# Last two blocks' outputs of an expert layer added through one-hot products, and the third output tile added onto a preset shift in memory

## Chip, cores and metric

The kernel runs on one core of a Trainium2 chip. The metric is the device time of one execution in microseconds (us), as the median of three runs. TensorE (PE) does the matrix products, VectorE (DVE), ScalarE (ACT) and GpSimd (POOL) the rest; SyncE (SP) issues most DMAs, POOL the indirect and the accumulating ones.

## What is computed

One step of a one-layer hybrid decoder over 512 prompt tokens and 8 sample tokens (520 rows, model width 2048), in float32. The part that matters is the end: a mixture of experts with two experts per token, and the last LayerNorm.

```python
h = silu(einsum('td,edf->tef', xf, w_gate)) * einsum('td,edf->tef', xf, w_up)
y = einsum('tef,te,efd->td', h, gate, w_down)
out = layer_norm(ALPHA * x1 + y, ln2_g, ln2_b)
```

## The kernel before

**Stages.** First comes the input projection with attention, recurrence and convolution beside it (lines 1805 and on), then the output projection, which ends in the first LayerNorm and the routing near 850 us, then the experts. The token rows chosen for one expert are cut into blocks of 128. A loop over blocks `j` gathers 128 rows, turns them, multiplies them with 8 tiles of gate and up weights and, one block later, with 4 tiles of down weights. In this run there are 17 blocks; in the code `last` is 16 and `nb` is 17. The last two blocks are written out behind the loop: `gate_up(last)`, then `down_column` four times for the block before, then four times for the last one, each for 512 of 2048 output columns.

**Precision.** A float32 product is made of three products of fp32r operands: each operand is split into a high part, which ACT writes (`bhi`, line 1050), and a low part, the difference, which DVE writes (`blo`, line 1683). Weights come by SP into `RAWB` (six slots of 1 MB, lines 602 and 682); SP reuses a slot when DVE has made the low part.

**Adding the outputs up.** `y_rows` is a table in device memory of 520 rows, preset with the scaled residual (line 659). After each block ACT copies the four finished PSUM banks to `YO` (line 1071), and POOL adds the 128 rows to their places in `y_rows` with one indirect accumulating DMA (line 768). For the second to last block this is done in four quarters of 512 columns, each as soon as it is copied (line 804). The last block's rows are not scattered: ACT copies them to `YO2`; DVE makes one-hot matrices `OWN` (lines 1737 to 1740) that say which output row each of the 128 rows belongs to; and PE multiplies `OWN` with `YO2` in plain float32 (lines 2266, 2268, 2275), which spreads the rows over the 512 prompt rows, in four tiles of 128, and over the 8 sample rows.

**The end.** SP waits for all scatters (line 704), then loads `y_rows` as four tiles `X2` of 1 MB (line 707) and the sample rows `X8` (line 709). Ahead of that it has loaded the LayerNorm rows, scale `LG2` and shift `LB2`, each as two DMAs of 64 partitions (lines 697 and 698), and `LG8`, `LB8` (line 701); all six DMAs count on one semaphore, `f_ln`, for which DVE waits before `centred(0)`. Per tile DVE adds the PE product to `X2` and sums the row (`added`, line 1767), ACT makes the mean (`mean`, line 1152), DVE subtracts it and applies the scale (`centred`, line 1772), ACT squares and sums (`squares`, line 1156) and takes the root (line 1157), and DVE inverts it (`root`, line 1776). Tiles 0 and 1 (`NACC = 2`) are finished by ACT (`scaled`, line 1161) and added by POOL onto output rows which SP has preset with the shift during the output projection (lines 624 and 625, accumulating DMA line 817). Tiles 2 and 3 are finished by DVE (`finished`, line 1785) and written plainly by SP (line 717). The sample rows take a side path through `Z8` and `z_rows` (lines 1144, 712, 714) and are written last (lines 1760, 719). Every engine takes its instructions in the order written; DMAs of one queue move in the order issued.

Of the kernel before, what the change touches and what calls it, by code (L numbers as in the profile page):

```python
# [16 lines left out]
D = 2048  # L17
# [97 lines left out]
def build(nc, a, o):  # L115
# [9 lines left out]
    y_quarters = y_rows.rearrange("t (c n) -> (t c) n", c=4)  # L125
# [93 lines left out]
    NF, NACC = 4, 2  # L219
# [5 lines left out]
    YO2 = sb("YO2", [128, D], F32, O_M + 8192)  # L225
    HTH2 = sb("HTH2", [128, 4, 128], F32R, O_M)
    HTL2 = sb("HTL2", [128, 4, 128], F32R, O_M + 2048)
    OWN = sb("OWN", [128, NF, 128], F32, O_M + 34816)
# [6 lines left out]
    OWN8 = sb("OWN8", [128, DB], F32, O_8 + 3584)  # L235
    TOKF = sb("TOKF", [128, 1], F32, O_8 + 3648)
# [28 lines left out]
    with ExitStack() as ctx:  # L265
# [165 lines left out]
        YIX4 = small("YIX4", [128, 4], I32)  # L431
# [33 lines left out]

        def last_bank(k, n):

            return ((0, 1, 2, 3), (6, 7, 4, 5))[k % 2][n]

        DOWN_BANK, LAST_DOWN_BANK = (2, 4, 5, 7), (0, 1, 3, 6)  # L470
# [20 lines left out]
        def _(sp):  # L491
# [160 lines left out]
            nb = sp.value_load(EBI[0:1, 31:32], min_val=7, max_val=MAXB - 2) + 2  # L652
# [40 lines left out]

            for k, (t, w) in enumerate(((LG2, "ln2g"), (LB2, "ln2b"))):
                sp.wait_ge(b_lo[k], 4 * nb - 1)
                passed(sp)
                sp.dma_start(t[0:64, :], a[w][0:64, :]).then_inc(f_ln, 16)
                sp.dma_start(t[64:128, :], a[w][0:64, :]).then_inc(f_ln, 16)
            sp.wait_ge(s_y0, 16 * NT)
            for t, w in ((LG8, "ln2g"), (LB8, "ln2b")):  # L700
                sp.dma_start(t[:, :], a[w][0:4, :].rearrange("r (c n) -> (r c) n", c=32)).then_inc(f_ln, 16)

            sp.wait_ge(f_out, 32 * NACC)
            sp.wait_ge(b_yw, 16 * nb + 48)
            passed(sp)
            for i in range(NF):
                sp.dma_start(X2[:, i, :], y_rows[128 * i:128 * i + 128, :]).then_inc(f_in[i], 16)
            in8 = "(g r) (c n) -> (r c) g n"
            sp.dma_start(X8[:, :, :], y_rows[SEQ:T, :].rearrange(in8, g=2, c=32)).then_inc(f_in8, 16)
# [17 lines left out]
        def _(pool):  # L727
# [17 lines left out]
            last_quarter = pool.to_reg(4 * T - 1)  # L745
# [72 lines left out]
            pool.wait_ge(b_yw, 16 * nb + 48 + 16 * NACC)  # L818
# [4 lines left out]
        def _(act):  # L823
# [312 lines left out]
            for n in range(1, 3):
                column_copy(n, n, nb, YO2, LAST_DOWN_BANK)
            act.activation(MV2[:, 0, 3:4], EPS_LN2, ACT.Sqrt)
            column_copy(3, 3, nb, YO2, LAST_DOWN_BANK)


            def samples_copy(n):
                act.wait_ge(f_p, 5 + n)
                act.activation(Z8[:, 512 * n:512 * n + 512], BANK[0:DB, last_bank(1, n), :], ACT.Copy).then_inc(b_y, 1)

            def samples_sd():
                act.wait_ge(f_t8, 2)
                act.activation(S8[:, 4:6], BANK[:, 7, 2:4], ACT.Sqrt, bias=EPS_LN2, scale=1.0 / D).then_inc(f_v8, 1)
# [26 lines left out]
            samples_sd()
# [3 lines left out]
        def _(dve):  # L1179
# [532 lines left out]
            with dve.Fori(1, MAXB) as j:  # L1712
                with dve.If(j < last):
# [653 lines left out]
```

## Time and profile before

| | |
|---|---|
| median of 3 runs | 1498.01 us (1496.25 to 1498.43) |
| profiled execution, its own time | 1493.46 us |
| span of the profiled execution | 1491.6 us |
| PE, DVE, ACT, POOL busy | 96%, 68%, 52%, 13% of the span |
| chain that ended last | PE 85%, DVE 7%, DMA 3%, ACT 2% |
| granted PE clock, mean | 0.982 |

The span runs from the first to the last instruction; the profiled execution's own time lies 1.9 us above it. The chain is the work that ended last, followed back from the end. PE holds it nearly throughout; the other shares gather at the stage borders and behind the last weight product. All stretches below are in us from the span's start.

### The profile page before, as it was taken

The page shows a single profiled execution, that of the slowest core. Times are in us where ns is not written, and L with a number is a line of the kernel's source. Part 1 is how long each engine was busy: PE and PEld are TensorE (multiplying, and loading weights), DVE is VectorE, ACT ScalarE, POOL GpSimd, SP SyncE. Part 2 cuts the span into 40 slices and gives each one's busy share as a digit, 9 for nine tenths or more (in the row PEclk, how much of TensorE's full clock was granted, in tenths as well). Part 3 has the DMA queues.
Part 4 walks back from the last instruction along what each step waited for, and adds up shares of the span by engine and source line. Part 5 has one row for each costly group of instructions (what it writes and reads, how often), then busy time and mean ns, then how long its engine had stood idle before and what let it go on. Part 6 is the DMA issues. An engine that isn't in the chain of part 4 may idle for free.

```text
span 1491.6 us, 24267 instructions
## 1 busy us (share of the span) xinstructions
PE 1439.3 (96%) x9396; PEld 1291.7 (87%) x9396; DVE 1015.0 (68%) x1287; ACT 770.8 (52%) x912; POOL 190.4 (13%) x99
## 2 busy tenths in 40 slices
PE   8999999999999999999997999999999999999995
PEld 7999999999999999999996467888888888888772
DVE  4246746757777787523125668888888888888877
ACT  4245545444434433411110047777777777777774
POOL 0000000000000000234330001121121211222130
PEclk9999999999999999999998899999999999999998
DMA  7321231322213312633435699999999999999997
GB/s 262 123 89 57 86 114 61 96 90 86 88 57 115 116 58 73 205 111 146 145 96 205 207 394 375 384 401 391 392 375 384 384 382 398 387 390 401 348 294 232
DMA packets 74389, 335.36 MB, mean 225 GB/s; under 512 B 12086, under 2 KB 18790, under 8 KB 45514
## 3 DMA queue, kind: packets, MB, share of 16 engines
q1 hardware_dynamic: 68842, 315.54, 56.2%
q0 software_dynamic: 5472, 18.74, 5.0%
q8 instruction: 56, 0.92, 0.2%
q14 instruction: 19, 0.16, 0.0%
HBM read 313.56 MB, written 40.73 MB: 238 GB/s over the span
## 4 chain that ended last, share of the span: by engine, by line
PE 85%; DVE 7%; DMA 3%; ACT 2%; issue 2%; POOL 0%; ACTq 0%; SPq 0%; DVEq 0%; POOLq 0%
PE BANK L1811 13%; PE BANK L1812 13%; PE BANK L1813 13%; PE BANK L2170 7%; PE BANK L2172 7%; PE BANK L2171 7%; PE BANK L2222 4%; PE BANK L2220 4%; PE BANK L2221 4%; PE BANK L2154 2%; DMA RAWB<-in_w_up 2%; PE BANK L2183 2%; PE BANK L1953 1%; PE BANK L1829 1%; PE BANK L2050 1%
## 5 line engine op out<-in xcount | busy, mean ns | idle before, releaser
L1811 PE MATMUL BANK<-XH,HI 128*128 128x260 f32 x1746 | 503.0, 288 | 1.4 <-DVE RT L1487 1.0
L1683 DVE TENSOR_TENSOR LOB<-RAWB,HIB 128x2048 fp32r<-128x2048 f32 x196 | 448.6, 2291 | 74.0 <-ACT HIB L1050 73.1
L1812 PE MATMUL BANK<-XL,HI 128*128 128x260 f32 x1746 | 495.3, 284 | 0.0
L1813 PE MATMUL BANK<-XH,LO 128*128 128x260 f32 x1746 | 494.3, 283 | 0.0
L1050 ACT ACTIVATE HIB<-RAWB 128x2048 fp32r<-128x2048 f32 x196 | 376.4, 1921 | 86.0 <-PE BANK L2172 66.1
L1811 PEld LDWEIGHTS BANK<-XH,HI 128*128 128x128 f32 x1746 | 331.2, 190 | 2.7 <-issue 1.7
L1812 PEld LDWEIGHTS BANK<-XL,HI 128*128 128x128 f32 x1746 | 331.1, 190 | 0.7
L1813 PEld LDWEIGHTS BANK<-XH,LO 128*128 128x128 f32 x1746 | 330.9, 190 | 0.0
L2170 PE MATMUL BANK<-HIB,XGH 128*128 128x512 f32 x512 | 201.8, 394 | 5.5 <-issue 3.0
L2172 PE MATMUL BANK<-LOB,XGH 128*128 128x512 f32 x512 | 200.0, 391 | 0.0
L2171 PE MATMUL BANK<-HIB,XGL 128*128 128x512 f32 x512 | 199.8, 390 | 0.0
L836 ACT ACTIVATE HI<-RAW 128x2048 fp32r<-128x2048 f32 x55 | 105.1, 1911 | 146.5 <-PE BANK L1813 139.6
L731 POOL TENSOR_TENSOR LO<-RAW,HI 128x2048 fp32r<-128x2048 f32 x14 | 66.1, 4721 | 713.5 <-ACT HI L836 713.5
L1198 DVE TENSOR_TENSOR LO<-RAW,HI 128x2048 fp32r<-128x2048 f32 x41 | 93.8, 2289 | 42.9 <-ACT HI L836 42.6
L2170 PEld LDWEIGHTS BANK<-HIB,XGH 128*128 128x128 f32 x512 | 96.7, 189 | 26.2 <-DVE LOB L1683 3.3
L2172 PEld LDWEIGHTS BANK<-LOB,XGH 128*128 128x128 f32 x512 | 96.5, 188 | 20.5
L1487 DVE SCALAR_TENSOR_TENSOR RT<-RT,BANK 128x260 f32<-128x260 f32 x32 | 13.5, 424 | 147.3 <-PE BANK L1813 147.3
L2171 PEld LDWEIGHTS BANK<-HIB,XGL 128*128 128x128 f32 x512 | 96.6, 189 | 19.5
L2220 PE MATMUL BANK<-HIB,HTH 128*128 128x512 f32 x240 | 99.4, 414 | 0.0
L2222 PE MATMUL BANK<-LOB,HTH 128*128 128x512 f32 x240 | 94.7, 395 | 0.0
L2221 PE MATMUL BANK<-HIB,HTL 128*128 128x512 f32 x240 | 93.6, 390 | 0.0
L768 POOL DMA_INDIRECT y_rows<-YO,YIXC x15 | 37.4, 2495 | 355.3 <-ACT YO L1071 355.3
(388 smaller groups left out, 1674.5 us busy)
## 6 DMA issues: line engine op xcount, KB each, us to landing
RAWB<-in_w_down SPq DMA_DIRECT2D x68, 1024.0 KB, 9.5
RAWB<-in_w_gate SPq DMA_DIRECT2D x67, 1024.0 KB, 9.4
RAWB<-in_w_up SPq DMA_DIRECT2D x67, 1024.0 KB, 8.9
RAW<-in_w_in SPq DMA_DIRECT2D x39, 1024.0 KB, 4.9
RAW<-in_w_out SPq DMA_DIRECT2D x16, 1024.0 KB, 5.0
Y<-in_xT SPq DMA_DIRECT2D x8, 520.0 KB, 9.1
RT<-in_xT SPq DMA_DIRECT2D x16, 260.0 KB, 5.2
x_rows<-R SPq DMA_DIRECT2D x5, 832.0 KB
```

The lines of the kernel that those rows point to most:

```text
L836: act.activation(HI[:, u % 2, :], RAW[:, u % 2, :], ACT.Copy).then_inc(s_hi, 1)
L1050: act.activation(HIB[:, s, :], RAWB[:, r, :], ACT.Copy).then_inc(b_hi, 1)
L1683: dve.tensor_tensor(LOB[:, s, :], RAWB[:, r, :], HIB[:, s, :].bitcast(F32), ALU.subtract).then_inc(b_lo[s], 1)
L1811: pe.matmul(bank, hw[:, c, :], h, start=(c == 0), stop=False)
L1812: pe.matmul(bank, hw[:, c, :], l, start=False, stop=False)
L1813: ins = pe.matmul(bank, lw[:, c, :], h, start=False, stop=(c == KC - 1))
L2170: pe.matmul(b, XGH[:, cc, :], hw[:, c, :], start=(cc == 0), stop=False)
L2171: pe.matmul(b, XGL[:, cc, :], hw[:, c, :], start=False, stop=False)
L2172: ins = pe.matmul(b, XGH[:, cc, :], lw[:, c, :], start=False, stop=(cc == KC - 1))
L2220: pe.matmul(b, th[:, c, :], hw[:, m, :], start=(c == 0), stop=False)
L2221: pe.matmul(b, tl[:, c, :], hw[:, m, :], start=False, stop=False)
L2222: ins = pe.matmul(b, th[:, c, :], lw[:, m, :], start=False, stop=(c == 3))
```

## The change

The last two blocks no longer differ: both outputs are split into high and low parts (`YAH`, `YAL` for the second to last, `YBH`, `YBL` for the last), and PE adds both through one-hot matrices `OWN[0]` and `OWN[1]`, which are now fp32r, with four fp32r products for each 512 columns. POOL's four quarter scatters go. DVE gets eight `out_lo` subtractions and a second set of one-hot matrices. SP loads `X2` and `X8` right behind the last weight tile, after a wait for the last scatter of the loop alone, and the LayerNorm rows after them. `NACC` is 3: output tile 2 too is preset in the output projection (one more pair of lines 624 and 625, with n = 9), scaled by ACT and added by POOL. The order of the last steps changes on PE, ACT and DVE. PSUM banks of the spread products are the down banks.

```diff
@@ -216,24 +215,27 @@
-    NF, NACC = 4, 2
+    NF, NACC = 4, 3
...
-    YO2 = sb("YO2", [128, D], F32, O_M + 8192)
+    YAH = sb("YAH", [128, D], F32R, O_M + 8192)
+    YAL = sb("YAL", [128, D], F32R, O_M + 16384)
+    YBH = sb("YBH", [128, D], F32R, O_M + 24576)
+    YBL = sb("YBL", [128, D], F32R, O_M + 32768)
...
-    OWN = sb("OWN", [128, NF, 128], F32, O_M + 34816)
+    OWN = [sb(f"OWN{x}", [128, NF, 128], F32R, O_M + 4096 + 2048 * i) for i, x in enumerate("AB")]
...
-    OWN8 = sb("OWN8", [128, DB], F32, O_8 + 3584)
-    TOKF = sb("TOKF", [128, 1], F32, O_8 + 3648)
+    OWN8 = [sb(f"OWN8{x}", [128, DB], F32R, O_8 + 3584 + 32 * i) for i, x in enumerate("AB")]
+    TOKF = sb("TOKF", [128, 2], F32, O_8 + 3648)
@@ -463,11 +464,11 @@
+DOWN_BANK, LAST_DOWN_BANK, STAT_BANK = (2, 4, 5, 7), (0, 1, 3, 6), 0
...
-    return ((0, 1, 2, 3), (6, 7, 4, 5))[k % 2][n]
...
-DOWN_BANK, LAST_DOWN_BANK = (2, 4, 5, 7), (0, 1, 3, 6)
+    return (DOWN_BANK, LAST_DOWN_BANK)[k % 2][n]
@@ -691,33 +693,31 @@
+    sp.wait_ge(s_y0, 16 * NT)
+    sp.wait_ge(b_yw, 16 * last)
...
+    for i in range(NF):
+        sp.dma_start(X2[:, i, :], y_rows[128 * i:128 * i + 128, :]).then_inc(f_in[i], 16)
+    in8 = "(g r) (c n) -> (r c) g n"
+    sp.dma_start(X8[:, :, :], y_rows[SEQ:T, :].rearrange(in8, g=2, c=32)).then_inc(f_in8, 16)
...
-    sp.wait_ge(s_y0, 16 * NT)
...
-    sp.wait_ge(f_out, 32 * NACC)
-    sp.wait_ge(b_yw, 16 * nb + 48)
...
-    for i in range(NF):
-        sp.dma_start(X2[:, i, :], y_rows[128 * i:128 * i + 128, :]).then_inc(f_in[i], 16)
-    in8 = "(g r) (c n) -> (r c) g n"
-    sp.dma_start(X8[:, :, :], y_rows[SEQ:T, :].rearrange(in8, g=2, c=32)).then_inc(f_in8, 16)
...
-    for k, (i, c0, n) in enumerate(((2, 0, D), (3, 0, D // 2), (3, D // 2, D // 2))):
+    for k, (i, c0, n) in enumerate(((3, 0, D // 2), (3, D // 2, D // 2))):
...
-    sp.wait_ge(f_out, 32 * NACC + 16 * (NF - NACC + 1) + 16)
+    sp.wait_ge(f_out, 32 * NACC + 32 * (NF - NACC) + 16)
@@ -788,23 +787,6 @@
-    pool.wait_ge(b_yw, 16 * last)
...
-    pool.tensor_copy(YIXC[:, :], YIX[:, bass.ds(last - 1, 1)]).then_inc(b_iy, 1)
-    pool.wait_ge(b_iy, last)
...
-    for n in range(4):
-        ins = pool.tensor_scalar(YIX4[:, n:n + 1], YIXC[:, :], 4, n, ALU.mult, ALU.add)
-    ins.then_inc(b_iy, 1)
-    pool.wait_ge(b_iy, last + 1)
...
-    for n in range(4):
-        pool.wait_ge(b_y, 4 * last - 1 + n)
...
-        pool.indirect_dma_start(
-            out=y_quarters, out_offset=bass.IndirectOffsetOnAxis(ap=YIX4[:, n:n + 1], axis=0),
-            in_=YO[:, 512 * n:512 * n + 512], in_offset=None,
-            bounds_check=last_quarter, oob_is_err=False, compute_op=ALU.add).then_inc(b_yw, 16)
@@ -815,7 +797,7 @@
-    pool.wait_ge(b_yw, 16 * nb + 48 + 16 * NACC)
+    pool.wait_ge(b_yw, 16 * last + 16 * NACC)
@@ -1121,31 +1103,31 @@
-    act.wait_ge(b_yw, 16 * last)
-    column_copy(0, 8, last)
+    column_copy(0, 8, last, YAH)
...
-    column_copy(1, 9, last)
+    column_copy(1, 9, last, YAH)
...
-    column_copy(2, 10, last)
+    column_copy(2, 10, last, YAH)
...
-    column_copy(3, 11, last)
+    column_copy(3, 11, last, YAH)
...
-    column_copy(0, 0, nb, YO2, LAST_DOWN_BANK)
+    act.wait_ge(b_yw, 16 * last)
+    column_copy(0, 0, nb, YBH, LAST_DOWN_BANK)
...
     for n in range(1, 3):
-        column_copy(n, n, nb, YO2, LAST_DOWN_BANK)
+        column_copy(n, n, nb, YBH, LAST_DOWN_BANK)
...
-    column_copy(3, 3, nb, YO2, LAST_DOWN_BANK)
+    column_copy(3, 3, nb, YBH, LAST_DOWN_BANK)
...
     def samples_copy(n):
-        act.wait_ge(f_p, 5 + n)
-        act.activation(Z8[:, 512 * n:512 * n + 512], BANK[0:DB, last_bank(1, n), :], ACT.Copy).then_inc(b_y, 1)
+        act.wait_ge(f_p, 9 + n)
+        act.activation(Z8[:, 512 * n:512 * n + 512], BANK[0:DB, last_bank(2, n), :], ACT.Copy).then_inc(b_y, 1)
...
-        act.activation(S8[:, 4:6], BANK[:, 7, 2:4], ACT.Sqrt, bias=EPS_LN2, scale=1.0 / D).then_inc(f_v8, 1)
+        act.activation(S8[:, 4:6], BANK[:, STAT_BANK, 2:4], ACT.Sqrt, bias=EPS_LN2, scale=1.0 / D).then_inc(f_v8, 1)
@@ -1161,17 +1143,18 @@
+    squares(0)
+    scaled(0)
+    mean(1)
     for n in range(4):
         samples_copy(n)
-    squares(0)
-    mean(1)
     squares(1)
-    scaled(0)
     mean(2)
+    scaled(1)
     squares(2)
-    scaled(1)
     mean(3)
     squares(3)
+    scaled(2)
     samples_sd()
 
 
@@ -1723,21 +1706,41 @@
+    def owners(k, x):
+        i = k - 1
+        if k == 0:
+            done(dve.tensor_copy(TOKF[:, x:x + 1], YIX[:, bass.ds(last - 1 + x, 1)]))
+        elif i < NF:
+            ts(OWN[x][:, i, :], IOS[:, :], float(CAP + 128 * i), TOKF[:, x:x + 1], ALU.add, ALU.is_equal)
+        else:
+            ins = ts(OWN8[x][:, :], IOS[:, 0:DB], float(CAP + SEQ), TOKF[:, x:x + 1], ALU.add, ALU.is_equal)
+            if x == 1:
+                ins.then_inc(f_add, 1)
...
+    def out_lo(n, j, lo, high, banks):
+        dve.wait_ge(b_y, 4 * j - 1 + n)
+        cols = slice(512 * n, 512 * n + 512)
+        dve.tensor_tensor(lo[:, cols], BANK[:, banks[n], :], high[:, cols].bitcast(F32), ALU.subtract).then_inc(b_xl, 1)
...
+        for x in range(2):
+            if 3 <= i < 3 + NF + 2:
+                owners(i - 3, x)
...
-    for n in range(3):
+    for n in range(2):
...
-    blo(3, 0, nb)
-    done(dve.tensor_copy(TOKF[:, :], YIX[:, bass.ds(last, 1)]))
-    for i in range(NF):
-        ts(OWN[:, i, :], IOS[:, :], float(CAP + 128 * i), TOKF[:, 0:1], ALU.add, ALU.is_equal)
-    ts(OWN8[:, :], IOS[:, 0:DB], float(CAP + SEQ), TOKF[:, 0:1], ALU.add, ALU.is_equal).then_inc(f_add, 1)
+    for n in range(2):
+        out_lo(n, last, YAL, YAH, DOWN_BANK)
+        blo(2 + n, 0, nb)
+    for n in range(2, 4):
+        out_lo(n, last, YAL, YAH, DOWN_BANK)
+    for n in range(4):
+        out_lo(n, nb, YBL, YBH, LAST_DOWN_BANK)
@@ -1763,8 +1766,8 @@
-            dve.wait_ge(f_p, 4 * (i + (i > 0)) + n + 1)
-            dve.scalar_tensor_tensor(X2[:, i, cols], X2[:, i, cols], 1.0, BANK[:, last_bank((0, 2, 3, 4)[i], n), :], ALU.mult, ALU.add,
+            dve.wait_ge(f_p, 4 * (i + (i > 1)) + n + 1)
+            dve.scalar_tensor_tensor(X2[:, i, cols], X2[:, i, cols], 1.0, BANK[:, last_bank((0, 1, 3, 4)[i], n), :], ALU.mult, ALU.add,
@@ -1787,17 +1790,17 @@
     added(0)
     dve.wait_ge(f_ln, 96)
     centred(0)
+    root(0)
     added(1)
-    root(0)
+    centred(1)
     added(2)
-    centred(1)
     root(1)
+    centred(2)
+    added(3)
+    root(2)
     samples_sum()
-    added(3)
+    centred(3)
     samples_centre()
-    centred(2)
-    finished(2, 1)
-    centred(3)
     finished(3, 2)
     samples_finish()
 
@@ -2260,25 +2263,45 @@
+    def first_part(bank, own, n):
+        cols = slice(512 * n, 512 * n + 512)
+        pe.matmul(bank, own[0], YAH[:, cols], start=True, stop=False)
+        pe.matmul(bank, own[0], YAL[:, cols], start=False, stop=False)
...
+    def second_part(bank, own, n):
+        cols = slice(512 * n, 512 * n + 512)
+        pe.matmul(bank, own[1], YBH[:, cols], start=False, stop=False)
+        pe.matmul(bank, own[1], YBL[:, cols], start=False, stop=True).then_inc(f_p, 1)
...
+    tile_own = [[w[:, i, :] for w in OWN] for i in range(NF)]
...
     for n in range(4):
-        pe.wait_ge(b_y, 4 * nb - 1 + n)
-        pe.matmul(BANK[:, last_bank(0, n), :], OWN[:, 0, :], YO2[:, 512 * n:512 * n + 512], start=True, stop=True).then_inc(f_p, 1)
+        pe.wait_ge(b_xl, 4 * nb + 1 + n)
+        first_part(BANK[:, last_bank(0, n), :], tile_own[0], n)
     for n in range(4):
-        pe.matmul(BANK[0:DB, last_bank(1, n), :], OWN8[:, :], YO2[:, 512 * n:512 * n + 512], start=True, stop=True).then_inc(f_p, 1)
-    for i in range(1, NF):
-        for n in range(4):
-            if i == 2:
-                pe.wait_ge(b_y, 4 * nb + 3 + n)
-            else:
-                pe.wait_ge(f_add, (2 + n) if i == 1 else (6 + n))
-            pe.matmul(BANK[:, last_bank(i + 1, n), :], OWN[:, i, :], YO2[:, 512 * n:512 * n + 512], start=True, stop=True).then_inc(f_p, 1)
+        pe.wait_ge(b_xl, 4 * nb + 5 + n)
+        second_part(BANK[:, last_bank(0, n), :], tile_own[0], n)
+    for n in range(4):
+        first_part(BANK[:, last_bank(1, n), :], tile_own[1], n)
+        second_part(BANK[:, last_bank(1, n), :], tile_own[1], n)
+    for n in range(4):
+        pe.wait_ge(f_add, 2 + n)
+        first_part(BANK[0:DB, last_bank(2, n), :], [w[:, :] for w in OWN8], n)
+        second_part(BANK[0:DB, last_bank(2, n), :], [w[:, :] for w in OWN8], n)
+    for n in range(4):
+        pe.wait_ge(f_add, 6 + n)
+        first_part(BANK[:, last_bank(3, n), :], tile_own[2], n)
+        second_part(BANK[:, last_bank(3, n), :], tile_own[2], n)
+    for n in range(4):
+        pe.wait_ge(b_y, 4 * nb + 3 + n)
+        first_part(BANK[:, last_bank(4, n), :], tile_own[3], n)
+        second_part(BANK[:, last_bank(4, n), :], tile_own[3], n)
...
-        pe.matmul(BANK[:, 7, 2 * k:2 * k + 2], ROWS[:, :], S8[:, 2 * k:2 * k + 2], start=True, stop=True).then_inc(f_t8, 1)
+        pe.matmul(BANK[:, STAT_BANK, 2 * k:2 * k + 2], ROWS[:, :], S8[:, 2 * k:2 * k + 2], start=True, stop=True).then_inc(f_t8, 1)
```

## Rows read from the trace of the kernel before

**Rows 1.** Chain of waits at the end: start us, us, what.

```profile
1446.28 8.68 DMA y_rows<-YO,YIX
...
1455.04 4.85 DMA X<-y_rows
...
1459.92 2.53 DVE X L1767 x8
```

**Rows 2.** Timeline of PE: start us, us, engine, line, operation.

```profile
1455.36 0.39 PE L2236 MATMUL BANK<-LOB,HTH 128*128 128x512 f32 x1
1455.59 3.59 PE L2266 MATMUL BANK<-YO,OWN 128*128 128x512 f32 x8
```

**Rows 3.** Timeline of DVE, same columns, idle time before in brackets.

```profile
1450.06 2.29 DVE L1683 TENSOR_TENSOR LOB<-RAWB,HIB 128x2048 fp32r<-128x2048 f32 x1 [0.43 <-ACT HIB L1050]
...
1452.45 0.87 DVE L1739 TENSOR_SCALAR OWN<-IOS,TOKF 128x128 f32<-128x128 f32 x4
...
1462.89 2.35 DVE L1772 SCALAR_TENSOR_TENSOR YA<-X,SM,LG 128x2048 f32<-128x2048 f32 x1 [0.45 <-ACT SM L1152]
1465.16 0.68 DVE L1767 SCALAR_TENSOR_TENSOR X<-X,BANK 128x512 f32<-128x512 f32 x1
...
1467.59 0.16 DVE L1776 RECIPROCAL SM<-SM 128x1 f32<-128x1 f32 x1
1467.98 0.69 DVE L1767 SCALAR_TENSOR_TENSOR X<-X,BANK 128x512 f32<-128x512 f32 x1 [0.23 <-DVE SM L1776]
...
1479.46 2.35 DVE L1785 SCALAR_TENSOR_TENSOR YA<-YA,SM,LB 128x2048 f32<-128x2048 f32 x1
...
1484.19 2.48 DVE L1785 SCALAR_TENSOR_TENSOR YA<-YA,SM,LB 128x1024 f32<-128x1024 f32 x2
```

**Rows 4.** Timeline of ACT, same columns.

```profile
1455.78 0.60 ACT L1071 ACTIVATE YO<-BANK 128x512 f32<-128x512 f32 x1 [0.60 <-PE BANK L2236]
...
1470.37 1.99 ACT L1161 ACTIVATE YA<-YA,SM 128x2048 f32<-128x2048 f32 x1
...
1477.11 2.00 ACT L1156 ACTIVATE SQ<-X,SM 128x2048 f32<-128x2048 f32 x1
...
1479.24 0.29 ACT L1157 ACTIVATE SM<-SM 128x1 f32<-128x1 f32 x1
```

**Rows 5.** Timelines of POOL and SP: DMA issues.

```profile
1473.00 0.93 POOL L817 DMA_DIRECT2D out_yp<-YA  x1 [23.75 <-ACT YA L1161]
...
1435.04 0.54 SPq L682 DMA_DIRECT2D RAWB<-in_w_down  x1
1438.33 0.54 SPq L697 DMA_DIRECT2D LG<-in_ln2g  x1
...
1481.84 5.19 SPq L717 DMA_DIRECT2D out_yp<-YA  x3
1487.63 0.38 SPq L719 DMA_DIRECT2D out_ys<-Q  x1
```

**Rows 6.** Stretches: PE, PEld, DVE, ACT, POOL busy, PEclk, DMA share, GB/s.

```profile
700.00:710.00 10.00, 10.00 (x96) 10.00 (x95) 6.02 (x11) 0.01 (x1) 4.59 (x1) 1.00 0.12 29
1436.00:1441.50 5.50, 5.50 (x27) 4.61 (x26) 5.07 (x3) 4.95 (x5) 3.22 (x2) 1.00 1.02 359
1441.50:1444.50 3.00, 3.00 (x15) 2.46 (x14) 2.35 (x2) 2.66 (x3) 1.84 (x2) 1.00 1.08 187
1457.00:1466.00 9.00, 9.00 (x22) 2.90 (x21) 5.63 (x12) 3.52 (x7) 0.00 (x0) 1.00 1.01 425
1474.50:1484.50 10.00, 0.59 (x2) 0.50 (x2) 9.83 (x16) 5.08 (x10) 0.86 (x1) 0.62 1.04 196
1485.50:1490.00 4.50, 0.00 (x0) 0.00 (x0) 2.03 (x5) 0.00 (x0) 0.00 (x0) 0.50 1.00 416
```

**Rows 7.** DMA queues in 1441.9 to 1451.9: packets, MB, share of 16 engines.

```profile
q1 hardware_dynamic: 435, 1.99, 87.6%
q0 software_dynamic: 329, 0.27, 16.0%
```

More of the change, by code:

```diff
@@ L124, in build @@
     y_rows = nc.dram_tensor("y_rows", [T, D], F32, kind="Internal").ap()
-    y_quarters = y_rows.rearrange("t (c n) -> (t c) n", c=4)
     z_rows = nc.dram_tensor("z_rows", [DB, D], F32, kind="Internal").ap()
@@ L430, in build @@
         YIXC = small("YIXC", [128, 1], I32)
-        YIX4 = small("YIX4", [128, 4], I32)
         EBC = small("EBC", [TT, MAXB + 1, 16])
@@ L651, in _ @@
             sp.wait_ge(r_idx, 1)
-            nb = sp.value_load(EBI[0:1, 31:32], min_val=7, max_val=MAXB - 2) + 2
+            last = sp.value_load(EBI[0:1, 31:32], min_val=7, max_val=MAXB - 2) + 1
+            nb = last + 1
             x1_out(0)
@@ L692, in _ @@
             down(nb, 0, True)
+            sp.wait_ge(s_y0, 16 * NT)
+            sp.wait_ge(b_yw, 16 * last)
+            passed(sp)
+            for i in range(NF):
+                sp.dma_start(X2[:, i, :], y_rows[128 * i:128 * i + 128, :]).then_inc(f_in[i], 16)
+            in8 = "(g r) (c n) -> (r c) g n"
+            sp.dma_start(X8[:, :, :], y_rows[SEQ:T, :].rearrange(in8, g=2, c=32)).then_inc(f_in8, 16)
             for k, (t, w) in enumerate(((LG2, "ln2g"), (LB2, "ln2b"))):
@@ L698, in _ @@
                 sp.dma_start(t[64:128, :], a[w][0:64, :]).then_inc(f_ln, 16)
-            sp.wait_ge(s_y0, 16 * NT)
             for t, w in ((LG8, "ln2g"), (LB8, "ln2b")):
                 sp.dma_start(t[:, :], a[w][0:4, :].rearrange("r (c n) -> (r c) n", c=32)).then_inc(f_ln, 16)
-            sp.wait_ge(f_out, 32 * NACC)
-            sp.wait_ge(b_yw, 16 * nb + 48)
-            passed(sp)
-            for i in range(NF):
-                sp.dma_start(X2[:, i, :], y_rows[128 * i:128 * i + 128, :]).then_inc(f_in[i], 16)
-            in8 = "(g r) (c n) -> (r c) g n"
-            sp.dma_start(X8[:, :, :], y_rows[SEQ:T, :].rearrange(in8, g=2, c=32)).then_inc(f_in8, 16)
             sp.wait_ge(b_y, 4 * nb + 6)
@@ L744, in _ @@
             last_token = pool.to_reg(T - 1)
-            last_quarter = pool.to_reg(4 * T - 1)
             def gather(j, rows, into=XG):
@@ L790, in _ @@
                     scatter(j)
-            pool.wait_ge(b_yw, 16 * last)
-            passed(pool)
-            pool.tensor_copy(YIXC[:, :], YIX[:, bass.ds(last - 1, 1)]).then_inc(b_iy, 1)
-            pool.wait_ge(b_iy, last)
-            passed(pool)
-            for n in range(4):
-                ins = pool.tensor_scalar(YIX4[:, n:n + 1], YIXC[:, :], 4, n, ALU.mult, ALU.add)
-            ins.then_inc(b_iy, 1)
-            pool.wait_ge(b_iy, last + 1)
-            passed(pool)
-            for n in range(4):
-                pool.wait_ge(b_y, 4 * last - 1 + n)
-                passed(pool)
-                pool.indirect_dma_start(
-                    out=y_quarters, out_offset=bass.IndirectOffsetOnAxis(ap=YIX4[:, n:n + 1], axis=0),
-                    in_=YO[:, 512 * n:512 * n + 512], in_offset=None,
-                    bounds_check=last_quarter, oob_is_err=False, compute_op=ALU.add).then_inc(b_yw, 16)
             pool.memset(ROWS[:, :], 0.0).then_inc(s_ones, 1)
@@ L1749, in samples_centre @@
                 dve.wait_ge(f_t8, 1)
-                done(ts(S8[:, 0:2], BANK[:, 7, 0:2], -1.0 / D, None, ALU.mult))
+                done(ts(S8[:, 0:2], BANK[:, STAT_BANK, 0:2], -1.0 / D, None, ALU.mult))
                 done(tt(X8[:, :, :], X8[:, :, :], S8[:, 0:2].unsqueeze(2).to_broadcast([128, 2, 64]), ALU.add))
```

## Prediction

> **What bounds the kernel now.** I read the page first: PE is busy 96% of the span, so a change behind the last weight product can only touch the last 36 us. Then the chain of waits from 1446 on: the last quarter scatter lands at 1454.96, the load of the first tile lasts until 1459.9, and from there DVE holds the chain to the end of its work [rows 1]. The timeline of PE says when the weight product ends: the next product stands 0.23 us behind its last one, at 1455.59 [rows 2]. So DVE starts 4.3 us behind that. The timeline of DVE gives prices: an added tile 2.53 [rows 1], a centred tile 2.27 (1462.89 to 1465.16), a gap of 0.45 for the mean where ACT must make it first, and 0.39 from one reciprocal to the next step [rows 3]. DVE is done at 1487.6, when the sample rows are issued [rows 5]; the span ends at 1491.6.
>
> Last, and what decides this case, the stretches by DMA rate [rows 6]. They show three rates with the DMA engines full each time: `X2` comes at 425 GB/s, POOL's two accumulating outputs go at 196, and the LayerNorm rows come at 187 as soon as the weights are through (1441.5 to 1444.5). Tile 2's plain output is issued at 1481.84 [rows 5], yet plain traffic at 416 GB/s shows only from about 1485. The end is thus bound by the DMA engines, which accumulate from about 1474.4 to 1485 and write plainly to about 1490.5.
>
> **The change, part by part.**
>
> *Preset of tile 2.* One more pair of 512 KB copies near 700 us. DMA is busy 12% there and PE is full for all 10 us [rows 6]. Cost nothing; without that cover it would be some 5 us of DMA, twice 1 MB at about 400 GB/s.
>
> *DVE before the tail.* Twelve small owner operations stand between weight subtractions; four such took 0.87 us [rows 3], so a pair costs some 0.4, and the idle time before a subtraction is 0.43 [rows 3]. They fit, with nothing over. Of the eight `out_lo`, two stand between the last subtractions. Nearest price: 0.61 each, the spacing of the 128x512 additions from PSUM (0.69 long) [rows 3]. Against 0.43 of idle each time, the last weight subtraction, which began at 1450.06 and took 2.29, moves by about 0.5 and ends near 1452.85. PE takes up the last tile at 1455.59 less 12 products of 0.227, or 1452.87. PE is 0 to 0.3 later; I take 0.1.
>
> *PE.* Four fp32r products for each 512 columns at 0.227 make 0.91; before it was two plain ones in 3.59 for four, or 0.9 [rows 2]. Tile 0 needs 16 products, 3.6 us, done near 1459.4. The second parts wait for ACT's last copy, which ends at 1456.4 [rows 4], plus one `out_lo`: 1457.1, in time. DVE's last addition of tile 0 ends at about 1460.35, plus 0.45 for the mean: DVE could centre at **1460.8**, against 1462.89 before. That is the gain of 2.1 us from the scatters and the load that go from the chain.
>
> *The transfers in the new order.* SP issues `X2` at about 1436, behind the last weight tile (1435.04 [rows 5]) and ahead of the scale and shift. The weights are through near 1441.9 (359 GB/s falls to 187 at 1441.5 [rows 6]). Then 4.2 MB at 425 take 9.9 us and the sample rows 0.6: 1452.4. Only now do 2.1 MB of LayerNorm rows come. In 10 us beside the scatters that queue moved 1.99 MB with 87.6% of the engines' time [rows 7], so 8.8 us of full time, or 9.2 for 2.1 MB. That ends at 1461.6. From issue to DVE's start the first `X2` tile took 4.85 [rows 1], 2.5 of it bytes at 425; of the other 2.4 I give 0.8 to the end. `centred(0)` waits for all of it: **S = 1462.5**. From below, if they came at 425 without the scatters: 4.9 us, 1458.1, no wait, S = 1460.8. From above, 187 throughout: 11.2 us, S = 1464.4. I take the value of rows 7, which covers nearly the whole transfer. This is a new wait, and the whole of DVE's remaining order is queued behind it; it eats 1.7 of the 2.1 us.
>
> The Trainium skill bears on why this load is slow (page "SBUF — State Buffer", section "Door 1: The DMA port swizzle"): a transfer on 64 partitions reaches half of the ports, and it gives 196 GB/s at 1 MiB for it. By that figure the load takes 10.7 us and S is 1463.9, and it would not get faster when the scatters go. The trace agrees, with 187 GB/s before the first scattered bytes showed.
>
> *DVE's tail, from S.* centred(0) 2.27; root 0.39; added(1) 2.5; mean gap 0.45; centred(1) 2.27; added(2) 2.5; root 0.39; gap 0.1; centred(2) 2.27; added(3) 2.5; root 0.39; sample sum 0.5; centred(3) 2.27: S+18.8. Sample step 1.1, root 0.2, two halves 2.4 [rows 3] and the last sample operations 1.0 give S+23.6. Before it was 24.7 from 1462.89. `finished(2)`, 2.3 us [rows 3], is gone, and half of it comes back as gaps, since DVE now stands closer behind ACT. PE keeps ahead: tile 3's products are done near S+11.7, wanted at S+13.1.
>
> *ACT and the accumulated tile 2.* ACT squares tile 3 from S+16.1; square and root take 2.4 (1477.11 to 1479.53) and `scaled(2)` 2.0 [rows 4]: S+20.5. Scaling tile 0 ended at 1472.36, POOL issued at 1473.00 to 1473.93 [rows 4, 5], and traffic began near 1474.4: 2.0 more; I take 1.9, S+22.4.
>
> *The last transfers.* Accumulating 1 MB at 196 GB/s takes 5.3 us. Tile 3's two halves, ready at S+21.3 and S+22.5, take 2.6 at 416 GB/s [rows 6], the sample rows 0.2. If the engines do one at a time, this is 8.1 us from S+22.4, and 0.8 until SP sees it: **S+31.3**. Before, the accumulated tiles were 0 and 1, and their 10.6 us lay beside DVE's work on tiles 2 and 3; now 5.3 us of accumulating stand behind the last ACT step. DVE ends 1.4 earlier (1486.1 for 1487.6), but the end lies 7.7 us behind DVE, not 4.0.
>
> **Sum.** 1462.5 + 31.3 = 1493.8 against a span of 1491.6: 2.2 us slower. The profiled execution's own 1493.46 becomes 1495.7. That execution was 4.5 us below the median of 1498.01, so against the median I add the same difference: 1500.2.
>
> **Rivals.**
>
> *A. Faster: neither the LayerNorm load nor the accumulating holds the end.* S is 1460.8 since the load speeds up without scatters, and plain outputs pass beside the accumulating one, which then ends alone at S+22.4+5.3+0.8 = S+28.5: 1489.3, 2.3 us faster. For it: two queues did share the engines in rows 7. Against it: while the second tile was accumulated, the plain one did not move. If in addition accumulating a lone tile costs little, DVE's end binds: 1460.8+23.6+4.0 = 1488.4, 3.2 faster. It decides from S below 1461.5 with both. Chance 0.12.
>
> *B. The load waits, the tail overlaps.* 1462.5+28.5 = 1491.0, 0.6 faster. Chance 0.13.
>
> *C. The load is in time, the tail does not overlap.* 1460.8+31.3 = 1492.1, 0.5 slower. Chance 0.12.
>
> *D. The load keeps its slowest rate.* S = 1464.4: 1495.7, 4.1 slower. For it: only 64 partitions at a time, and no other queue is needed to make it slow. Chance 0.17.
>
> *E. The change doesn't come to act*, since `X2` is held back by something ahead of it on SP and lands as late as before: then `centred(0)` is at 1462.9 and the long tail remains, 1494.2. It is near my forecast in time; chance 0.03. The forecast itself has 0.43.
>
> **How the numbers follow.** A measurement of this kernel can tell about 0.2%, 3.0 us, from no change. Slower by more than that: D nearly whole (0.15) and 0.2 of the forecast and E, where 0.8 us more does it, and spread between runs: 0.33. Faster: a third of A, and spread and what I have not seen: 0.13. The rest, 0.54, is within it. The range goes from B with run spread (2 us below 1498.0) to D with a margin for a PE held up by DVE (5.2 above): 1496.0 to 1503.2.
>
> **What would show it.** Right: `X2` traffic directly behind the weights at above 400 GB/s and done by 1453; a wait of DVE before `centred(0)` whose releaser is a DMA, 1 to 3 us long, with `centred(0)` near 1462.5; the third POOL output issued near 1483.5 and 5 us of DMA at half rate behind it; DVE done 5 us or more before the end. Wrong: `centred(0)` near 1460.8 with no wait (rate of the LayerNorm load above 300), or plain output moving at above 200 GB/s beside the accumulating one, or a gap of PE above 0.5 us before its last weight tile, or PE's spread products holding DVE.

## The result and the profile after

| | before | after |
|---|---|---|
| median of 20 runs, us | 1497.52 (1494.12 to 1503.73) | 1504.51 (1500.65 to 1507.58) |
| ratio, 95% interval | | 1.0043 [1.0033, 1.0052] |
| span of the profiled execution | 1491.6 | 1504.1 |
| P: end of the last weight product | 1455.59 | 1462.65 |
| from P to the end of the span | 36.0 | 41.45 |

The change makes the kernel 0.43% slower, some 6.4 us. The forecast was 2.2 us and a range that ended at 1503.2; the median of 1504.51 lies outside it. Whole profiled executions of one kernel differ by several us ahead of P (last section), so all readings are made from P, which is found as in [rows 2], here by the first row that reads `YAH`:

```profile
1462.42 0.39 PE L2239 MATMUL BANK<-LOB,HTH 128*128 128x512 f32 x1
1462.65 0.39 PE L2268 MATMUL BANK<-YAH,OWNA 128*128 128x512 f32 x1
```

Chain of waits at the end, as [rows 1]:

```profile
1450.28 20.97 DMA LB<-in_ln2b
1471.27 2.35 DVE YA L1775
1473.93 2.53 DVE X L1770 x8
...
1491.00 2.48 DVE YA L1788 x2
```

No scatter and no `X2` is in it now; a load from `in_ln2b` stands there for 21 us, and DVE takes over at 1471.27. Its issue at 1450.28 is none of the big rows: it is `LB8`, the 32 KB that only the sample rows need (line 709 of the kernel after). DVE's timeline, as [rows 3], shows the wait itself:

```profile
1463.48 0.69 DVE L1723 TENSOR_TENSOR YBL<-BANK,YBH 128x512 fp32r<-128x512 f32 x1 [0.91 <-ACT YBH L1053]
1465.19 0.69 DVE L1770 SCALAR_TENSOR_TENSOR X<-X,BANK 128x512 f32<-128x512 f32 x1 [1.02 <-PE BANK L2274]
...
1471.27 2.35 DVE L1775 SCALAR_TENSOR_TENSOR YA<-X,SM,LG 128x2048 f32<-128x2048 f32 x1 [3.56 <-DMA LB<-in_ln2b]
...
1494.12 0.29 DVE L1763 TENSOR_TENSOR Q<-X,LB 128x128 f32<-128x128 f32 x1
```

`added(0)` begins at P+2.54, waits for PE alone, and is over by P+5.1; `centred(0)` begins at P+8.62, against P+7.30 in [rows 3]. DVE is done at 1494.4, P+31.8, about where it was before (P+32.0). All the rest is behind it. The issues on ACT, POOL and SP, as [rows 4, 5]:

```profile
1443.46 2.88 SPq L700 DMA_DIRECT2D X<-y_rows  x4
...
1449.01 0.60 SPq L707 DMA_DIRECT2D LB<-in_ln2b  x1
1449.65 0.58 SPq L709 DMA_DIRECT2D LG<-in_ln2g  x1
1450.28 2.06 SPq L709 DMA_DIRECT2D LB<-in_ln2b  x1
...
1492.32 1.53 SPq L717 DMA_DIRECT2D out_yp<-YA  x2
1494.44 1.10 SPq L719 DMA_DIRECT2D out_ys<-Q  x1
```
```profile
1491.72 0.85 POOL L799 DMA_DIRECT2D out_yp<-YA  x1 [6.74 <-ACT YA L1143]
```

How long these loads took from issue to landing, of those issued in 1446 to 1450.5 (KB each, median us):

```profile
LG<-in_ln2g SPq DMA_DIRECT2D x2, 512.0 KB, 17.8
LB<-in_ln2b SPq DMA_DIRECT2D x2, 512.0 KB, 20.1
LB<-in_ln2b SPq DMA_DIRECT2D x1, 32.0 KB, 21.0
```

Taken one by one, the last half of the scale row `LG2` landed at 1466.3 (issued 1447.74, 18.6 us), the last half of the shift row `LB2` at 1469.0 (1449.01, 20.0 us), and `LB8` at 1471.25. DVE waits for all six since they count on one semaphore, but `centred(0)` reads the scale row alone, which was there 4.9 us before DVE went on.

And the stretches by rate, as [rows 6], same columns; the last block is the queues' rows of 1492.7 to 1500.0, as [rows 7]:

```profile
1448.50:1458.50 10.00, 10.00 (x46) 8.29 (x45) 9.23 (x7) 8.22 (x8) 0.00 (x0) 1.00 1.02 428
1459.20:1464.20 5.00, 5.00 (x23) 4.14 (x23) 4.06 (x7) 2.69 (x4) 0.00 (x0) 1.00 1.00 209
1464.20:1468.00 3.80, 3.80 (x18) 3.14 (x17) 2.52 (x8) 0.25 (x2) 0.00 (x0) 1.00 0.99 220
1468.00:1469.00 1.00, 1.00 (x7) 0.81 (x6) 0.00 (x0) 0.97 (x2) 0.00 (x0) 1.00 0.59 151
1469.00:1470.00 1.00, 1.00 (x6) 0.74 (x5) 0.00 (x0) 1.00 (x2) 0.00 (x0) 1.00 0.28 76
1492.70:1500.00 7.30, 0.00 (x0) 0.00 (x0) 1.65 (x5) 0.00 (x0) 0.00 (x0) 0.50 0.97 210
1500.00:1502.30 2.30, 0.00 (x0) 0.00 (x0) 0.00 (x0) 0.00 (x0) 0.00 (x0) 0.50 0.75 276
1502.30:1504.10 1.80, 0.00 (x0) 0.00 (x0) 0.00 (x0) 0.00 (x0) 0.00 (x0) 0.50 0.00 0
```
```profile
q0 software_dynamic: 128, 1.05, 79.2%
q1 hardware_dynamic: 117, 0.48, 17.3%
```

`X2` goes at 428 GB/s directly behind the weights and is through by 1459. The LayerNorm rows follow at 209 to 220 until about 1469. What fades out behind them until 1470.5 is mostly `LG8` and `LB8`: in 1469.0 to 1470.5, 129 of 136 packets are below 512 bytes. At the end the third accumulated tile (q0) and the plain halves (q1) share the engines, which are full all the same, and nothing moves in the last 1.8 us. The last 0.9 us of bytes (1501.4 to 1502.3) is mostly small packets again, 253 of 254 below 512 bytes for 0.06 MB, from the sample rows' output.

### The profile page after: what moved, and what is told of

Read it like the earlier page. It is cut to its first block, busy times and chain, and to the rows that moved or that the text cites. A ratio compares the mean times of both kernels' runs of the same rounds, so it can differ in the third digit from the quotient of the medians.

```text
span 1504.1 us, 24348 instructions
## 1 busy us (share of the span) xinstructions
PE 1444.9 (96%) x9436; PEld 1301.6 (87%) x9436; DVE 1017.6 (68%) x1300; ACT 773.2 (51%) x913; POOL 182.9 (12%) x91
## 4 chain that ended last, share of the span: by engine, by line
PE 84%; DVE 7%; DMA 4%; ACT 2%; issue 2%; SPq 0%; ACTq 0%; DVEq 0%
PE BANK L1814 13%; PE BANK L1815 13%; PE BANK L1816 13%; PE BANK L2173 7%; PE BANK L2175 7%; PE BANK L2174 7%; PE BANK L2225 4%; PE BANK L2223 4%; PE BANK L2224 4%; DMA RAWB<-in_w_up 2%; PE BANK L2157 2%; PE BANK L1956 1%; DMA LB<-in_ln2b 1%; PE BANK L1832 1%; PE BANK L2186 1%
```

## The experiments

Each kernel was timed in rounds with the kernel before. "Stretch" is the time from P to the end of the span in its profile. Unless it says otherwise, a kernel is told by its edit to the kernel after. The main lines of each edit are printed; what only follows from them (SP's list of outputs, the counts in waits) mostly is not.

**a1: two accumulated tiles.** `NACC` back to 2; DVE finishes tile 2, SP writes it.

```diff
-    NF, NACC = 4, 3
+    NF, NACC = 4, 2
-    scaled(2)
-    root(2)
+    finished(2, 1)
```

> The changed kernel with two accumulated tiles again; tile 2 is finished by DVE and written plainly. Counted from the end of the last weight product (P), the kernel before ended at P+36.0 and the changed one at P+41.4. Theory 1 (the last accumulating transfer holds the end): DVE gets 2.3 us more work, yet the end moves up, to about P+38; 3 to 4 us faster than the changed kernel, 2 to 3 us slower than the kernel before (ratio about 1.002). Theory 2 (only the late LayerNorm rows matter, the tail is bound by DVE): 2 us slower than the changed kernel, ratio near 1.006.

Measured: 1.0008 [0.9994, 1.0022], stretch 37.61, as its first theory said. The late loads cost even more than in after (`centred(0)` at P+9.85 behind a wait of 4.80; it was P+8.6), and yet the end is 3.8 us nearer to P. So most of the loss is in the third accumulated tile.

**a2: LayerNorm rows ahead of `X2`.**

```diff
-    for i in range(NF):
-        sp.dma_start(X2[:, i, :], ...)
     for k, (t, w) in enumerate(((LG2, "ln2g"), (LB2, "ln2b"))):
         ...
+    for i in range(NF):
+        sp.dma_start(X2[:, i, :], ...)
```

> The changed kernel with the LayerNorm rows loaded ahead of the y tiles, three accumulated tiles kept. Theory 1 (the wait of centred(0) is that load's place in the queue): no DMA wait before centred(0), which starts at P+5.3 instead of P+8.6, and the end at P+38, 3.3 us faster than the changed kernel. Rival (the y tiles now come late instead, since the slow rows hold the queue): added(0) waits for its tile and centred(0) starts at P+7 or later, gain below 1.5 us.

Measured: 1.0014 [1.0001, 1.0028], stretch 38.43. DVE's timeline:

```profile
1465.82 0.69 DVE L1770 SCALAR_TENSOR_TENSOR X<-X,BANK 128x512 f32<-128x512 f32 x1 [1.24 <-DMA X<-y_rows]
...
1468.79 2.35 DVE L1775 SCALAR_TENSOR_TENSOR YA<-X,SM,LG 128x2048 f32<-128x2048 f32 x1 [0.45 <-ACT SM L1134]
```

The wait for the LayerNorm loads is gone. `added(0)` now waits for `X2`, but only 0.2 us longer than it waited for PE. `centred(0)` is at P+5.72, 2.9 us earlier, and the whole stretch is 3.0 shorter.

**a3: both, a1 and a2.**

> Both: LayerNorm rows first and two accumulated tiles, so only the one-hot products and the early y loads are left of the change. Theory 1: centred(0) at P+5.3, end at P+34.5, 1.5 us faster than the kernel before (ratio 0.999). Rival (the one-hot part costs PE or DVE time ahead of P, or the remaining order is slower): ratio 1.001 or more although the tail after P is shorter.

Measured: 0.9993 [0.998, 1.0006], stretch 36.68, against 36.0 of before. The two losses account for 4.8 of the 5.4 us of the stretch, and the runs can't tell the rest from nothing. But the earlier start still brings nothing, where the end was expected at P+34.5. DVE's timeline says why: the sample rows' side path is next.

```profile
1489.43 0.29 DVE L1747 TENSOR_TENSOR X<-X,W 128x128 f32<-128x128 f32 x1 [3.16 <-DMA W<-z_rows]
```

**a4: the kernel before with three accumulated tiles**, nothing else of the change.

```diff
-    NF, NACC = 4, 2
+    NF, NACC = 4, 3
+    scaled(2)
-    finished(2, 1)
+    root(2)
```

> The kernel before with three accumulated tiles and nothing else of the change. Theory 1: the last accumulating transfer stands behind the last ACT step, end near P+39.5 instead of P+36.0, ratio about 1.0023. Theory 2 (DVE bound): DVE is relieved of 2 us, end near P+34, ratio about 0.9987.

Measured: 1.0043 [1.0027, 1.0059], stretch 39.96, 4.0 more than before. DVE is done at 1490.1, P+29.9, and the end lies 10 us behind it. The stretches by rate:

```profile
1485.00:1491.00 6.00, 0.00 (x0) 0.00 (x0) 5.00 (x8) 1.32 (x2) 0.85 (x1) 0.50 1.03 212
1491.00:1497.00 6.00, 0.00 (x0) 0.00 (x0) 0.00 (x0) 0.00 (x0) 0.00 (x0) 0.50 0.99 286
```

DVE's work on the tile is saved (it was done at P+32.0), but the engines are full until 1497, 7 us behind DVE. This part alone is as slow in the runs as the whole change, although its stretch is only 4.0 us longer, not 5.4; the other 2.4 us of its 6.4 (interval 4.0 to 8.8) aren't explained.

**a5: a3 with the samples' steps later**, so that DVE doesn't stand before `W<-z_rows`. `part(3, k)` finishes one half of tile 3.

```diff
     centred(2)
     added(3)
-    samples_sum()
     finished(2, 1)
     centred(3)
+    samples_sum()
+    root(3, None)
+    part(3, 0)
     samples_centre()
-    finished(3, 2)
+    part(3, 1)
     samples_finish()
```

> The kernel with LayerNorm rows first and two accumulated tiles (one-hot products kept), where DVE waited 3.2 us for the sample rows from memory ahead of centring tile 3; here tile 3 is centred first and the sample steps stand between its later parts. Theory 1 (that wait is the next thing that holds DVE): DVE done near P+31.8 instead of P+34.1, end near P+34.8 instead of P+36.7; 1.2 us faster than the kernel before (ratio 0.998 to 0.999). Rival (the plain outputs behind the second accumulating one hold the end): end stays at P+36 or later.

Measured: 0.9991 [0.9976, 1.0006], stretch 33.27, 3.4 shorter than a3 and 2.7 shorter than before, 1.5 better than expected; `centred(0)` stayed at P+5.51. The same kernel again:

**a10**

> The kernel with norm rows first, two accumulated tiles and the samples' steps later, once more. Its ratio was 0.9991 with an interval that takes in 1. If the 2.7 us by which its stretch behind the last weight product is shorter than before's (33.3 against 36.0) is what the runs have too, the ratio is 0.998 again, and its stretch 33.3. Rival: the shorter stretch is given back ahead of it, by the rows' loads and the one-hot products in the last blocks, and the ratio is 1.000 or above.

Measured: 0.9989 [0.9974, 1.0005], stretch 33.29. Either interval takes in 1. The order of a5 was not put into the kernel before, so how much of the 2.7 us is the one-hot products' and how much the order's isn't shown.

**a6: after, with tile 2 written plainly by POOL** over the preset (so its output lacks the shift).

```diff
-    in_=YA[:, i, :], accum_op=ALU.add)
+    in_=YA[:, i, :], **({} if i == 2 else dict(accum_op=ALU.add)))
```

> The changed kernel in which POOL writes output tile 2 plainly instead of adding it, so that its shift is left out; all else, the issuing engine too, as it is. Theory 1 (accumulating moves bytes at half rate and the engines take one thing at a time): 2.6 us of transfer for 5.3, end at P+38.7 instead of P+41.4, ratio to the kernel before 1.0025. Rival (the late issue behind ACT costs it, not the adding): end moves less than 0.7 us.

Measured: 1.0011 [0.9999, 1.0023], stretch 37.52, 3.9 less than after. From `centred(0)` to the end it is 28.3, against 32.8. The stretch of the last transfers:

```profile
1490.00:1493.00 3.00, 0.00 (x0) 0.00 (x0) 0.19 (x1) 0.00 (x0) 0.00 (x0) 0.50 1.00 399
```

The same bytes, issued by POOL behind the same step of ACT, but at 399 GB/s, save 4.5 us: it is the accumulating that costs, not POOL, the queue or ACT's lateness. It costs more than the 2.6 or 2.7 us that were expected from bytes by rate: in after the accumulating queue took 5.8 us of the engines' full time (79.2% of 7.3) where 1 MB at 399 takes 2.6, and the rest of the 4.5 lies in engines that weren't full and in the time behind the last bytes.

**a7: after, with each LayerNorm row in one transfer of 128 partitions.**

```diff
-    sp.dma_start(t[0:64, :], a[w][0:64, :]).then_inc(f_ln, 16)
-    sp.dma_start(t[64:128, :], a[w][0:64, :]).then_inc(f_ln, 16)
+    sp.dma_start(t[:, :], a[w][:, :]).then_inc(f_ln, 16)
...
-dve.wait_ge(f_ln, 96)
+dve.wait_ge(f_ln, 64)
...
-    "ln2g": np.broadcast_to(A(ln2_g)[0], (TT, D)),
-    "ln2b": np.broadcast_to(A(ln2_b)[0], (TT, D)),
+    "ln2g": np.broadcast_to(A(ln2_g)[0], (128, D)),
+    "ln2b": np.broadcast_to(A(ln2_b)[0], (128, D)),
```

> The changed kernel with scale and shift rows each loaded by one transfer of 128 partitions instead of two of 64 (the host lays the same row out 128 times instead of 104); order as in the change, behind the y tiles. Theory 1 (half of the partitions give half of the rate): the 2.1 MB come at above 400 GB/s, in 5 us instead of 10, no DMA wait before centred(0), which starts at P+5.5, end at P+38.2; ratio 1.002. Rival (the source rows or the place in the queue make it slow): rate near 200 GB/s and centred(0) at P+8.6 as before.

Measured: 1.002 [1.0008, 1.0032], stretch 38.24, 3.2 less than after. The rows' stretch:

```profile
1462.00:1463.00 1.00, 1.00 (x6) 0.84 (x5) 1.00 (x2) 0.98 (x2) 0.00 (x0) 1.00 1.10 453
1463.00:1464.00 1.00, 1.00 (x6) 0.81 (x5) 1.00 (x3) 0.99 (x2) 0.00 (x0) 1.00 0.98 410
```

The same bytes go at over 400 GB/s, still behind `X2`, and `centred(0)` is at P+5.51 with no wait for a transfer. So the slow rate comes from the form of the load and not from scatters or from its place in the queue; the wait needs both the slow form and the late place, since a2 removes it too. The Trainium skill (page "SBUF — State Buffer", section "Door 1: The DMA port swizzle") says that a transfer on 64 partitions reaches half of the ports; 209 to 220 against 410 to 453 GB/s agrees. The edit also makes two transfers of four and reads 128 rows of the source instead of the same 64 twice; these were not tried apart from the partitions.

**a8: after, without the preset of tile 2** (whose output is then added onto whatever lies in memory).

```diff
-    if i < NACC:
+    if i < 2:
```

> The changed kernel without the preset of output tile 2 in the output projection, so that its shift is left out and the tile is added onto what lies in memory. Prediction's claim (the pair of copies is hidden): time as the changed kernel, ratio to the kernel before 1.0036 to 1.0043. Rival (the copies delay the output projection or what follows by a microsecond or more): ratio 1.003 or less.

Measured: 1.004 [1.0021, 1.0059], stretch 40.90, against 1.0043 for the whole change. The interval leaves room for 2 us either way; the traces are sharper. In 705 to 720 the preset raises the DMA share from 0.30 to 0.46, and PE does 138 products with it (a6) as without it (a1, a5, a10). The preset is hidden.

**a9: a5 with the whole rows of a7.**

> The kernel with norm rows first, two accumulated tiles and the samples' steps later, and the two norm rows loaded by one transfer of all 128 partitions each. In that kernel centred(0) already had its row at 5.51 us behind the end of the last weight product with no wait for a transfer, and the span ended 33.27 us behind it. If the late rows are all that the form of their load costs, nothing is left to gain: centred(0) at 5.5, the end at 33.3, ratio to before 0.998 to 0.999. Rival: the whole rows free the queue earlier for X2, which added(0) waits for, and give 0.5 to 1 us more (end at 32.5, ratio 0.9975).

Measured: 0.9971 [0.9957, 0.9985], stretch 33.25. The same kernel again:

**a11**

> The kernel with norm rows first as whole rows, two accumulated tiles and samples later, once more; its ratio to before was 0.9971 [0.9957, 0.9985] and its stretch behind the last weight product 33.25 us, 2.76 shorter than before's, which would make 0.9982. If the stretch is all that differs, the ratio is 0.998 again and the end at 33.25. Rival: 0.9971 was luck and it is no better than the kernel with halves of 64 rows (0.9991 and 0.9989): 0.999.

Measured: 0.9982 [0.9968, 0.9997], stretch 33.37. Both intervals lie below 1: this version beats both kernels, by some 0.2 to 0.3%. That the whole rows themselves add to a5 isn't shown, since the stretches are equal and the intervals overlap; by its stretch alone it should give 1 less 2.7 in 1497.5, or 0.9982.

**a12: the kernel before with whole rows.**

> The kernel before, with each of the two norm rows loaded by one transfer of all 128 partitions and nothing else changed. There the rows move while the last scatters and weights are still going on and nobody waits for them, so the form of the load should be hidden: the end 36.0 us behind the last weight product, ratio 1.000. Rival: the half-rate loads hold back the last weight tile or a quarter scatter in before too, and the kernel gains 0.5 to 1 us: ratio 0.9995 or less, with added(0) earlier than 4.33.

Measured: 0.9995 [0.9979, 1.0011], stretch 35.09, so the trace went the rival's way by 0.9 us (`added(0)` begins at P+1.14), too little for the runs to tell. Chain of waits, and POOL's last quarter scatter and SP's issue of `X2` in the timelines:

```profile
1457.37 3.43 PE BANK L2265 x8
1460.80 3.53 PE BANK L2267 x8
1464.33 7.08 PE BANK L2274 x16
```
```profile
1447.90 2.06 POOL L803 DMA_INDIRECT y_rows<-YO,YIX  x1 [0.68 <-issue]
```
```profile
1452.32 1.97 SPq L706 DMA_DIRECT2D X<-y_rows  x4
```

SP issues `X2` 4.4 us behind the last scatter's issue; in [rows 1] it was 8.8. So half of that link of the old chain went with the slow row load, and this small edit takes `X2` from the chain. The chain then goes through PE's plain float32 products, and little is won: the second `centred` step is at P+14.84 and DVE is done at P+32.0, both as in before. An earlier `X2` alone is worth nothing to DVE in this order of steps. The 0.9 us stand at the end: the first accumulating output is issued at P+16.8 instead of P+17.4, and from 1477 to 1491 the DMA engines are full (share 1.01).

**All stretches against all ratios.** The difference of the stretch from before's 36.0, over 1497.5, beside what the runs gave:

| kernel | stretch | would give | measured |
|---|---|---|---|
| after | 41.45 | 1.0036 | 1.0043 [1.0033, 1.0052] |
| a1 two accumulated | 37.61 | 1.0011 | 1.0008 |
| a2 rows first | 38.43 | 1.0016 | 1.0014 |
| a3 both | 36.68 | 1.0004 | 0.9993 |
| a4 before, three | 39.96 | 1.0026 | 1.0043 [1.0027, 1.0059] |
| a5, a10 samples later | 33.27, 33.29 | 0.9982 | 0.9991, 0.9989 |
| a6 third plain | 37.52 | 1.0010 | 1.0011 |
| a7 whole rows | 38.24 | 1.0015 | 1.0020 |
| a8 no third preset | 40.90 | 1.0033 | 1.0040 |
| a9, a11 | 33.25, 33.37 | 0.9982 | 0.9971, 0.9982 |
| a12 before, whole rows | 35.09 | 0.9994 | 0.9995 |

The stretch behind P, from one execution each, explains every ratio within its interval, but for a4, which misses by 0.0001. Nothing that the change does ahead of P has to be assumed to cost anything; but the intervals reach 1.4 to 2.9 us to either side, so a cost of 1 us there would not show.

## Why the prediction was wrong

The direction, the two waits and the place of each were right; the range failed since two terms of the sum were too small, and both errors add up. The first is S, the start of `centred(0)`: the forecast counted 2.1 MB of rows and gave nothing to the two small loads that count on the same semaphore. The second is the last transfers, put at 8.1 plus 0.8 us and measured at 9.6 plus 1.8. By its steps, in times from P (P was 1455.59 in its sum):

- **DVE ahead of the tail, and PE: right.** The `out_lo` fit. From PE's idle time of 2.97 us at the loop's exit to P it took 45.69 us before and 45.73 in a10, which has this part of the change; 0.1 was allowed. `added(0)` is done at P+5.1 and would let `centred(0)` go at P+5.5 (a5, a7), where 5.2 was forecast.
- **The preset: right.** Hidden (a6, a8).
- **The transfers in the new order: S was 1.7 us too early.** The issue of `X2` and its 428 GB/s came as written. S was put at 1462.5, P+6.9; it was P+8.6. The rows themselves were sized well: the forecast gave them 9.2 and 0.8 behind, 10.0 in all, and they took 9.8, from 1459.2 to the landing of the shift row at 1469.0, which is P+6.4. The failed step is "`centred(0)` waits for all of it" with "all" counted as the 2.1 MB of rows. The wait takes in `LG8` and `LB8` too, 32 KB each in small packets, and the last of them landed 2.2 us behind the rows (2.1 to 2.6 in after, a1, a6 and a8). That size is a reading of the trace: no run took these two off the semaphore. One execution gives S only roughly: with the loads in the same order it was P+8.3 in a8, P+9.2 in a6 and P+9.9 in a1.
- **Rival D** (the slowest rate, S at P+8.8, chance 0.17) had the time of S by luck. Its reason was half right: a7 shows that the form of the load sets the rate, with no scatter needed. But the rows went at 209 to 220 GB/s, not 187, and landed when the value of [rows 7] said.
- **DVE's tail from S: right.** 23.6 forecast (its items add up to 23.5), 23.1 measured (1471.27 to 1494.41).
- **ACT and the accumulated tile: nearly right.** S+22.4 forecast for the first bytes; they come near S+21.4 (1492.7).
- **The last transfers: mis-sized.** 8.1 plus 0.8 forecast; measured are 9.6 (1492.7 to 1502.3) plus 1.8. q0 needed 79.2% of 7.3, 5.8 us of full time, where 5.3 was written; the engines were a quarter idle in the last 2.3 us, of which the sample rows' small packets took 0.9 at a share of 0.31, where 0.2 was written; and the end lay 1.8 us behind the last bytes, not 0.8. So S to the end is 32.8 where 31.3 was forecast. "If the engines do one at a time" was right for the total: plain and accumulating bytes overlapped (which rivals A and B built on), but a shared engine's time was not saved by it.
- **Sum:** 1.7 and 1.5 too small: 5.4 us for 2.2. The runs give 6.4, with an interval from 4.9 to 7.8.
- **Chances:** "within 0.2%" had 0.54 and was wrong, the slower side 0.33. Both errors lie in one direction since a queue's time was taken as bytes by rate, without its small packets and its uneven finish.
- **What made the whole change lose** was seen in the prediction as two separate effects. The experiments rank them: in stretches, the third accumulated tile costs 4.0 us by itself (a4) and 3.8 in the whole (a1), the late loads 3.0 to 3.2 (a2, a7; both together 4.8, a3), and what is left of the change gains 2.7 once neither is there and DVE's steps for the samples are moved (a5), behind a wait that the prediction never named.

## What to carry to other kernels

A transfer that was hidden keeps its full price when the work above it moves: read the rate at which it goes alone, ask whether its form (64 partitions here) sets that rate, and put it ahead of what needs it later. Ask too which of the loads on a semaphore the next step really needs. Here one wait stands for six loads, and the step needs the scale row, which landed at P+3.7 (1466.3); with a semaphore of its own it could have begun at P+5.5, as in a5 and a7. That is an estimate from the landings of the profile; no run tried it.

Don't move work from a computing engine to an accumulating write near the end: 1 MB that saves 2 us of DVE (a4) took 5.8 us of full DMA engines there, and written plainly it came out 4.5 us shorter (a6). Whether the earlier accumulating writes, of tiles 0 and 1, are free was not tried. In before the engines are full from there to the end ([rows 6]), so they may well cost something too.

For the end of a queue, add to bytes by rate the small packets and the uneven finish: 2.2 us behind the rows here, and 2.5 more than forecast in the last transfers.

## What was unexpected of the hardware

**PE's clock falls for short stretches in some executions.** The granted clock of PE was 0.89 in after (first block) and 1.00 in before (second block) at the same PE work near 710 us, and 0.67 against 1.00 behind the idle time at the loop's exit:

```profile
705.00:720.00 15.00, 15.00 (x122) 15.00 (x122) 5.86 (x11) 1.92 (x1) 2.69 (x1) 0.89 0.46 176
1416.00:1420.00 4.00, 4.00 (x14) 3.15 (x13) 2.89 (x2) 0.04 (x1) 0.00 (x0) 0.67 0.77 301
```
```profile
705.00:720.00 15.00, 15.00 (x135) 15.00 (x135) 6.33 (x12) 1.92 (x1) 4.19 (x1) 1.00 0.30 107
1410.00:1414.00 4.00, 4.00 (x18) 3.29 (x19) 2.73 (x2) 1.04 (x1) 0.00 (x0) 1.00 0.94 365
```

14 products for 18 in equal time: part of the 4 us went at 1.2 GHz instead of 2.4. Near 710 us it isn't the preset's doing: a4 and a6, with the same preset, show a clock of 1.00 in 705 to 720, and a9, without it, shows 0.89. From the exit to P it takes 45.7 us in before, a6, a9 and a10, 47.1 to 47.4 in after, a1 to a5, a11 and a12, and 48.5 in a7 and a8: three levels that go with no part of the change, since before's code stands on both of the first two (before, a12). The profiled executions reach P between 1455.6 and 1465.1; these levels make 2.8 us of that, the 13 products fewer near 710 us (122 for 135) another 1.4, and the rest wasn't traced. What decides it in an execution stays open. It is why one profile's span (12.5 us longer after) must not be compared as it stands.

**Two full queues do share.** In [rows 6] the plain output seemed to wait for the accumulating ones: none of its bytes moved until 1485.0, 3.2 us behind its issue. In after the first plain bytes came 1.5 us behind their issue, in between the accumulating ones: in 1496.7 to 1498.7 the plain queue moved 0.19 MB and the accumulating one 0.37. Which of the two orders occurs was not tried.
